# First loads, two orders in attentions, and 512-column slabs over half of the rows in a retention

## The reference, cut to what matters

```python
# first block, layer 0
proj = rms_norm(h, norm_mix_g[0]) @ ab_w_in[0]           # qa ka va qb kb vb
qa, ka = rope(rms_norm(qa)), rope(rms_norm(ka))
o_a = softmax(qa @ ka.T * scale) @ va                    # 8 heads
o_b = dilated_attention(qb, kb, vb, rel_bias)            # 8 heads, bias by distance
h = h + concat(o_a, o_b) @ ab_w_out[0]
...
# second block, layer 0: differential attention, 8 heads with two softmaxes each
a = p[:, :, 0] - lmbda * p[:, :, 1]
o = rms(a @ v, subln) * (1 - lam_init)
...
# second block, layer 1: retention, 4 heads, keys 256 wide, values and gates 512 wide
q, k, v, g = split(rms(h, mix_norm[1]) @ rt_w_in)
o = rms((q @ k.T * decay) @ v, subln)                    # causal
m = (silu(g) * o) @ rt_w_out
```

## Time and profile before

| | us |
|---|---|
| three timed executions | 1643.93, 1644.05, 1644.21 (median 1644.05) |
| profiled execution, its own time | 1644.38 |
| span of the core in it | 1642.3 |
| PE busy | 1629.2 |
| DVE busy | 1052.2 |
| ACT busy | 852.0 |
| POOL busy | 47.6 |

### The profile page before, as it was taken

One profiled execution on the slowest core, in us unless ns is written; L12 is line 12 of the kernel. 1 busy time (PEld: TensorE's weight loads), 2 busy tenths in 40 slices (PEclk: granted clock), 3 DMA queues, 4 the chain that ended last, 5 costly groups with the idle time before them and its releaser, 6 DMA issues.

```text
span 1642.3 us, 24239 instructions
## 1 busy us (share of the span) xinstructions
PE 1629.2 (99%) x9546; PEld 1398.1 (85%) x9546; DVE 1052.2 (64%) x1199; ACT 852.0 (52%) x1078; POOL 47.6 (3%) x50
## 2 busy tenths in 40 slices
PE   9999999999999999999999999999999999999999
PEld 7878888867888888889988888888889999888887
DVE  6766556777665676667776666666666444466665
ACT  5655444665444464455775544554445454455443
POOL 1100000000000030000100000000000000000000
PEclk9999999999999999999999999999999999999999
DMA  9535544314545454544444554454545444435540
GB/s 369 182 129 193 205 184 178 151 67 178 203 181 204 179 194 180 203 179 180 141 160 165 202 205 179 180 211 180 192 181 209 154 159 175 156 152 205 205 179 26
DMA packets 42575, 293.72 MB, mean 179 GB/s; under 512 B 4721, under 2 KB 5025, under 8 KB 8450
## 3 DMA queue, kind: packets, MB, share of 16 engines
q1 hardware_dynamic: 39168, 281.04, 45.9%
q0 software_dynamic: 2752, 10.58, 1.8%
q10 hardware_dynamic: 578, 0.99, 0.2%
HBM read 289.44 MB, written 3.15 MB: 178 GB/s over the span
## 4 chain that ended last, share of the span: by engine, by line
PE 90%; DVE 5%; ACT 2%; issue 2%; POOL 0%; ACTq 0%; DVEq 0%; POOLq 0%
PE ups L271 26%; PE accs L250 14%; PE accs L252 14%; PE accs L251 14%; PE ups L269 11%; DVE wlo L244 2%; PE ups L274 2%; ACT whi L240 1%; DVE h L673 1%; PE ups L409 1%; PE ups L453 1%; PE ups L411 1%; PE ups L406 1%; PE ups L2288 1%; PE ups L1348 1%
## 5 line engine op out<-in xcount | busy, mean ns | idle before, releaser
L244 DVE TENSOR_TENSOR wlo<-raw,whi 128x2048 fp32r<-128x2048 f32 x265 | 609.2, 2301 | 223.1 <-ACT whi L240 223.1
L271 PE MATMUL ups<-xhl,whi 128*128 128x512 f32 x1824 | 634.2, 396 | 0.0
L240 ACT CAST whi<-raw 128x2048 fp32r<-128x2048 f32 x265 | 505.2, 1909 | 79.4 <-PE accs L252 79.4
L269 PE MATMUL ups<-xhl,wlo 128*128 128x256 f32 x1596 | 445.1, 279 | 0.0
L271 PEld LDWEIGHTS ups<-xhl,whi 128*128 128x128 f32 x1824 | 331.1, 188 | 64.2
L269 PEld LDWEIGHTS ups<-xhl,wlo 128*128 128x128 f32 x1596 | 300.9, 189 | 10.1
L250 PE MATMUL accs<-whi,hidh 128*128 128x512 f32 x692 | 271.7, 393 | 0.0
L252 PE MATMUL accs<-whi,hidl 128*128 128x512 f32 x692 | 269.5, 389 | 0.0
L251 PE MATMUL accs<-wlo,hidh 128*128 128x512 f32 x692 | 269.3, 389 | 0.0
L250 PE MATMUL accs<-whi,xhl 128*128 128x256 f32 (+1 forms) x576 | 177.1, 307 | 0.3 <-DVE xhl L2138 0.3
L252 PE MATMUL accs<-whi,xhl 128*128 128x256 f32 (+1 forms) x576 | 171.6, 298 | 0.0
(11 more groups left out here) (268 smaller groups left out, 1610.8 us busy)
## 6 DMA issues: line engine op xcount, KB each, us to landing
raw<-weights SPq DMA_DIRECT2D x265, 1024.0 KB, 4.8
gain<-gains POOLq DMA_DIRECT2D x9, 512.0 KB, 4.0
rel_scratch<-sub_rstd POOLq DMA_DIRECT2D x1, 2048.0 KB, 15.5
big<-rel_scratch POOLq DMA_DIRECT2D x1, 1536.0 KB, 10.7
h<-x_in SPq DMA_DIRECT2D x2, 512.0 KB, 4.3
raw<-weights SPq DMA_DIRECT2D x2, 512.0 KB, 6.6
tabs<-consts POOLq DMA_DIRECT2D x1, 1024.0 KB, 7.2
tabs<-consts ACTq DMA_DIRECT2D x1, 512.0 KB, 9.4
```

Of the source, the lines that this page charges most:

```text
L240: nc.scalar.copy(whi[:, m % SPLIT, :], raw[:, m % RAW, :]).then_inc(hi_ready, 1)
L244: nc.vector.tensor_tensor(wlo[:, m % SPLIT, :], raw[:, m % RAW, :], whi[:, m % SPLIT, :].bitcast(F32), ALU.subtract).then_inc(lo_ready, 1)
L269: nc.tensor.matmul(bank[:, 0:T], W(wlo, n, k, j * P, (j + 1) * P), xh[:, k, :], start=False, stop=False)
L271: mm = nc.tensor.matmul(bank, W(whi, n, k, j * P, (j + 1) * P), xhl[:, :, k, :], start=k == 0, stop=k == KC - 1)
```

## The change

**First loads.** ACT loads the identity first and then the gains broadcast to 128 partitions (512 KB). The one-row matmuls and the spread gains in PSUM are gone, and `stay_warm` is one group of 12. DVE makes the first piece of `xn` in two halves, and `turn_part(0)` waits for the first alone. SP loads the first half of slab 0 between the two pieces of `h`. ACT and DVE take their first steps in another order. POOL issues the loads for the bias table ahead of the rotation's table.

**First attention.** POOL rotates `q1` ahead of its wait for the stored bias table. ACT does `turned_copy(0)` ahead of `high(5)`.

**Differential attention.** ACT does `prob_copy(1)` ahead of `high(7)`; DVE does `o_low(2)` and `combined(7)` ahead of `low(14)`.

**Retention.** A value or gate slab holds 512 columns of half of the rows: slab j = 0 (4) rows 0 to 511, j = 1 (5) rows 512 to 1023. Each takes 2 token blocks x 4 row blocks x 3 = 24 matmuls of 512 columns, and the two slabs fill two banks, one for each token block (`pair_of`). DVE takes both value banks after j = 1, and ACT both gate banks after j = 5, at the start of the next head.

```diff
@@ turn_part @@
-            pe.wait_ge(xn_ready, 3 * q + (1 if b < 2 else b))
+            if q == 0 and b == 0:
+                pe.wait_ge(S("first_xn"), 1)
+            else:
+                pe.wait_ge(xn_ready, 3 * q + (1 if b < 2 else b))
@@ raw_scalar, q == 0 @@
-                take_high(act, q, (0, 1))
+                take_high(act, q, (0,))
                 first_high(act, 0)
-                take_high(act, q, (2, 3))
+                take_high(act, q, (1, 2, 3))
@@ gain_piece @@
+            if q == 0 and p == 0:
+                half = slice(0, D // 2)
+                nc.vector.tensor_tensor(xn[:, half], h[:, 0, half], gain[:, half], ALU.mult
+                                        ).then_inc(S("first_xn"), 1)
+                lo = D // 2
@@ norm_vector, q == 0 @@
+                take_low(dve, q, (0,))
                 gain_piece(dve, q, s, 1)
                 gain_piece(dve, q, s, 2)
-                take_low(dve, q, (0, 1))
                 first_low(dve, 0)
-                take_low(dve, q, (2,))
+                take_low(dve, q, (1, 2))
@@ ab_scalar @@
+            turned_copy(0)
             high(5)
-            turned_copy(0)
@@ da_scalar @@
+            prob_copy(1)
             high(7)
-            prob_copy(1)
@@ da_vector @@
             biased(7)
+            o_low(2)
+            combined(7)
             low(14)
-            combined(7)
-            o_low(2)
             low(15)
@@ rt_tensor @@
+        def pair_of(u, j):
+            first = 2 * (u % 2) if j in (0, 1, 4, 5) else 2 - 2 * (u % 2)
+            return accs[:, first, :], accs[:, first + 1, :]
+            def bank_free(u, j):
+                if j == 0 and u >= 1:
+                    pe.wait_ge(S("rt_taken"), 4 * u - 2)
+                if j in (2, 3) and u >= 1:
+                    pe.wait_ge(S("rt_taken"), 4 * u)
+                if j == 4:
+                    pe.wait_ge(S("rt_v"), u + 1)
+            def tokens_part(n, s, t, bank, rows):
+                for k in rows:
+                    mm = three(bank, xh[:, 4 * s + k, t * P:(t + 1) * P], xl[:, 4 * s + k, t * P:(t + 1) * P],
+                               W(whi, n, k, 0, 512, 512), W(wlo, n, k, 0, 512, 512),
+                               s == 0 and k == 0, s == 1 and k == 3)
+                return mm
@@ rt_scalar @@
+                if j == 0 and u >= 1:
+                    gates(u - 1)
                 if j == 1 and u >= 1:
                     stats(u - 1)
...
+                if j == 4:
+                    bring_table(ACT.Silu)
@@ rt_vector @@
-                if j < 2:
+                if j == 1:
+                    if u >= 1:
+                        gated(u - 1)
                     dve.wait_ge(slab_used, n_r + m + 1)
...
                     for t in range(TB):
-                        ins = nc.vector.tensor_scalar(v_rt[:, u % 2, t, j * T:(j + 1) * T],
-                                                      rt_bank(m)[:, t * T:(t + 1) * T], rt_square[:, t:t + 1], None,
-                                                      ALU.mult)
+                        ins = nc.vector.tensor_scalar(v_rt[:, u % 2, t, :], pair_of(u, 0)[t], rt_square[:, t:t + 1],
+                                                      None, ALU.mult)
@@ sync @@
+            sp.dma_start(h[:, 0, :], x[0, 0:P, :]).then_inc(x_loaded[0], 16)
             sp.dma_start(raw[:, 0, 0:SLAB // 2], weights[0][:, 0:SLAB // 2]).then_inc(S("first_half"), 16)
+            sp.dma_start(h[:, 1, :], x[0, P:T, :]).then_inc(x_loaded[1], 16)
@@ gpsimd @@
             pool.wait_ge(x_loaded[0], 16)
             pool.dma_start(rope_rows[:, :], rope_gain.broadcast_to([P, 4 * HD])).then_inc(S("rope_rows"), 16)
+            pool.wait_ge(xn_ready, 3)
+            pool.dma_start(rel_sb[:, :].rearrange("p (c h) -> p c h", h=B_HEADS),
+                           rel_bias.unsqueeze(1).broadcast_to([NB, COPIES, B_HEADS])).then_inc(S("rel_loaded"), 16)
+            pool.dma_start(hot_sb, consts[0:NB, C_HOT:C_HOT + REL]).then_inc(S("rel_loaded"), 16)
+            pool.dma_start(cnt_sb, consts[:, C_CNT:C_CNT + REL]).then_inc(S("rel_loaded"), 16)
             pool.wait_ge(S("rope_rows"), 16)
@@ scalar @@
-            act.dma_start(gain[0:1, :], gains[0:1, :]).then_inc(S("first_gain"), 16)
             act.dma_start(ident, consts[:, 0:P]).then_inc(mats_loaded, 16)
+            act.dma_start(gain[:, :], gains[0:1, :].broadcast_to([P, D])).then_inc(S("first_gain"), 16)
@@ tensor @@
-            stay_warm(WARM // 2)
-            pe.wait_ge(filled, 3)
-            pe.wait_ge(S("first_gain"), 16)
-            for a in range(2):
-                mm = nc.tensor.matmul(accs[:, 2 + a, :], one_row[:, :], gain[0:1, a * 512:(a + 1) * 512],
-                                      start=True, stop=True)
-            mm.then_inc(S("gain_spread"), 1)
-            stay_warm(WARM // 2)
+            stay_warm(WARM)
```

More of the change, by code:

```diff
@@ L2357, in high_pair, with gates @@
                 ins.then_inc(S("r_high"), 1)
+            def gates(u):
+                act.wait_ge(slab_used, n_r + RT_SLABS * (u + 1))
+                if u == 0:
+                    act.wait_ge(rstd_ready, ROOTS[9] + 1)
+                if u >= 2:
+                    act.wait_ge(S("r_gated"), u - 1)
+                for t in range(TB):
+                    nc.scalar.activation(gate_rt[:, u % 2, t, :], pair_of(u, 4)[t], ACT.Silu, scale=rstd[:, t:t + 1]
+                                         ).then_inc(S("rt_taken"), 1)
             raw_root_scalar(act, 9)
@@ L2708, in in_slabs, with row_slabs @@
     return w.reshape(KC, P, n, IN_W).transpose(2, 1, 0, 3).reshape(n, P, SLAB)
+def row_slabs(w):
+    return w.reshape(2, KC // 2, P, 2 * IN_W).transpose(0, 2, 1, 3).reshape(2, P, SLAB)
 def out_slabs(w):
```

76 lines of the change are left out of this document (29 added, 47 removed).

## The result

| | before | after |
|---|---|---|
| median of 5 runs beside each other, us | 1644.21 | 1635.92 |
| span of the profiled execution, us | 1642.3 | 1633.8 |

What follows compares the result with a forecast made beforehand. TensorE, busy 99% of the span, was taken as the bound. Start and table 2.0, copy 0.6, rotation 1.3, differential attention 1.2 and retention 4.9 sum to 10.0 us, from a median of 1644.05 to 1634.1, range 1631.5 to 1638.0.

Steps and rivals of the forecast that it cites:

- What bounds it: Whole kernel: TensorE is busy for 99% of the span, so only its own stream and its rare idle places count.
- Retention, 4.9: Value and gate slabs: 24 matmuls of 512 columns replace 48 of 256, 5.2 us saved less 0.3 at breaks.
- Differential attention, 1.2: Two TensorE waits closed by reordering: 0.4 us at `prob_copy(1)` and 0.8 at `o_low(2)`; bounds 0.4 and 1.5.
- `turned_copy(0)`, 0.6: First attention: with ACT's copy ahead of the split of slab 5, TensorE's wait of 0.64 us goes, 0.6 gained.
- Start and table, 2.0: First loads: earlier first projection and no wait for the bias table give 2.0 us together; bounds 0.5 and 3.3.
- I take 5.3, so it lands at 6.6: Start: the 512 KB gains load takes 5.3 us from issue and lands at 6.6; bounds 5.3 and 7.9.
- By that rule the new gaps between the transposes cost nothing: Start: transposes don't count as activity for TensorE's clock, so new gaps between them cost nothing.
- What is late next: DVE's rotation: First queries, near 34.8 us: DVE's rotation comes forward by only 1.7 to 2.2, so 2.0 us, not 2.4.
- The rotation, 1.3: First attention: POOL's earlier rotation closes TensorE's 1.62 us wait, less 0.3 for ACT; bounds 0.6 and 1.9.
- ends at 47.2: First attention: POOL's rotation starts at 43.2 and ends at 47.2, old time axis, before TensorE is ready at 49.3.
- Rival 2: Start gives 0.5; DVE's `low(5)`, stretched 1.7 us by POOL's rotation, holds TensorE about 1.0: sum 7.5, 1636.6 us; 22%.
- the forecast's own case: Whole kernel: all terms as forecast, sum 10.0 us, median 1634.1; terms reach from 1632.5 to 1636; 53%.

Runs made afterwards that it cites:

- experiment 5: The changed kernel with the three loads of the bias table back behind GpSimd's four products: 1636.2 us.
- experiment 1: The kernel before with the wide retention slabs alone: 1639.6 us, a ratio of 0.9974 to before.
- experiment 2: The changed kernel with the start of before (one gain row spread by TensorE, old load and cast orders), early bias table loads kept: 1636.2 us.
- experiment 3: The changed kernel with 24 instead of 12 matmuls on zeros ahead of the transposes and 6 more between their second and third groups: 1635.46 us.
- experiment 8: The changed kernel with DVE's subtraction for slab 5 put behind the maxima and probabilities of heads 2 and 3: 1634.84 us.
- experiment 9: The changed kernel with GpSimd's rotation of the second half of the queries again behind the toeplitz read: 1641.0 us, ratio to before 0.9980.
- experiment 7: The changed kernel with the second piece of `h` ahead of the first half of slab 0 on SP's queue: 1636.0 us.
- experiment 10: The changed kernel with the two orders in the differential attention as before: 1637.2 us.

## Why the prediction was right, and where it was off

- **What bounds it** held: TensorE's stream, and only its rare waits. Every experiment that gained closed one of them or made one earlier.
- **Retention, 4.9**: right, at 4.7. The pitch was the one taken from another stage. 0.5 instead of 0.3 is missing from the 5.2; that it went at the breaks was not separated. No wait came up.
- **Differential attention, 1.2**: slightly low, 1.5 in the trace. `prob_copy(1)` gave 0.6 where I put 0.4, `o_low(2)` 0.9 where I put 0.8; part of the idle time there came back as the new wait of 0.28.
- **`turned_copy(0)`, 0.6**: right, at 0.7.
- **Start and table, 2.0**: the step that failed. It gave 0.9 (0.2 start, 0.7 table). Three terms were wrong, and one more was added up wrongly.
  - "I take 5.3, so it lands at 6.6": the load took 6.7 us, the upper bound, and the transposes began at 8.86 instead of 7.3, the first projection at 13.57 instead of 12.2, slab 1 at 20.34 instead of 18.8; the prediction named 8 us as the point from which the start fails, and it was 7.92. Its landing of the second piece of `h`, 9.1, was right (8.88) and set nothing.
  - "By that rule the new gaps between the transposes cost nothing": zeros in these gaps and ahead of them brought slab 1 forward by 1.06 us, of the 1.5 that it was late.
  - "What is late next: DVE's rotation": right as a place, but it was taken to move with the start by 1.7 to 2.2. It hung on slab 3's load over the cast on ACT, so that even 3.1 us of earlier start gave nothing. I followed DVE's chain back to its own work and not to the load behind ACT's cast, which the change's own early table loads had pushed from 17.8 to 21.5 us.
  - Start and table were added up, where at this place either alone gives what both give (experiment 5).

  Behind the second term stood a rule of the Trainium skill (TensorE: Matmul & The Clock Gate, Part 4: PE-mode transpose), that transposes are no activity for the clock. The traces neither show nor refute it: in before all 16 transposes kept a pitch of 0.21 us, but in experiments 1 and 2 it fell to 0.11 in their midst, with no other matmul between them. What I drew from it was wrong in any case, since the gaps around the transposes could be filled, and were in experiment 3.
- **The rotation, 1.3**: 0.8. The step was "ends at 47.2", on the old time axis; with the 0.9 us by which this work came earlier that is 46.3, and it ended at 48.4, 2.1 later. Rival 2 had the mechanism, with the roles changed: `low(5)` was hardly stretched (0.37 us, not 1.7), but GpSimd's addition stood while DVE subtracted. The Trainium skill's rule of the shared SBUF interfaces (GPSIMD Engine Reference, 1. Specifications) agrees with experiment 8: 1.29 us apart from that subtraction, 3.19 beside it. I had priced it as a rival at 22%, with 1.0 us of TensorE's time, which is what experiment 8 gave back.
- **The sum** was 1.7 too large: 1.1 of start and table, 0.5 of the rotation, 0.2 of the retention, 0.3 and 0.1 the other way in the differential attention and at the copy; the rest lies between trace and times. What happened is rival 2, with the load behind ACT's cast as a second reason for its first half: its 1636.6 is nearer to 1635.9 than the forecast's 1634.1. So the number held because 4.7 of the 8.3 us rest on a pitch that was read from rows; of the smaller terms ahead of it, the forecast's own case did not happen.

## What to carry to other kernels

Before an earlier start is counted, follow the next waiting engine back through every instruction that stands ahead in its queue, to the DMA: a cast that waits for a load three slabs on can hold a small root that everybody needs. Take such small steps ahead of work that waits for data. And when a GpSimd step is moved, look at what DVE does in its new place: here the same move was worth 1 us more with one subtraction put elsewhere. Loads that are issued earlier delay others that are still under way: the bias table's made slab 3 land some 3 us later. And a long wait of TensorE costs more than its length: behind the 4.30 us of experiment 9 the lower clock took another 1.5.

## What the runs showed of the hardware that I had not expected

- GpSimd's elementwise instruction was held for most of a DVE subtraction of two SBUF inputs: 3.19 us instead of 1.29 in eight kernels out of eight, and DVE lost 0.37 on 2.29. With a small DVE instruction it is the other way: 128x2 elements took 2.44 us under the rotation, 0.50 in experiment 8, and 0.17 where GpSimd stood still.
- TensorE's clock rose at another moment from execution to execution of the same start. The 16 transposes from 10.23 on took 3.52 us in before, 2.87 in experiment 1 and 2.17 in experiment 2, with the same instructions ahead of them. In after it was at its upper level at the end of the zeros (the last at a pitch of 0.22 us), and at the lower one again after 2.8 us of idle time; in experiment 7 the same zeros ran at the lower level to their last (a pitch of 0.43), the first eight transposes, behind 2.4 us of idle time, at the upper, and the second eight, behind another 1.5, at the lower. Slab 1 of five kernels with the same start (after and experiments 5, 8, 9, 10) began between 19.6 and 20.3 us; slab 3's load levelled that to within 0.2 us by slab 4.
- A broadcast load that writes 512 KB from a row of 4 KB is no cheaper than 512 KB of data: 6.7 us here, where its neighbours of the same size took 3.8 to 9.9, and 4.0 later in the kernel; and what is issued beside it took 0.9 to 2.1 us longer (experiment 7 against experiment 2).
